# The first body of a hybrid RG-LRU and convolution block: the pair of ma in front of xa

## The reference

```python
h = concatenate([meta, x])                       # 16 + 512 tokens
hn = rms_norm(h, norm_g)
xa, sa, vb, gb, sb, ma, mb = split(hn @ w_in)
ya = rg_lru(causal_depthwise_conv(xa, conv_a_w, conv_a_b), w_rg, b_rg, w_ig, b_ig, lam) * silu(sa)
yb = silu(layer_norm(causal_depthwise_conv(vb * sigmoid(gb), conv_b_w, conv_b_b))) * silu(sb)
merged = sigmoid(ma) * (ya @ w_proj_a) + sigmoid(mb) * (yb @ w_proj_b)
out = rms_norm(h + merged @ w_out)[:, 16:]       # the meta tokens are dropped again
```

## Time and profile before

| what | value |
| --- | --- |
| median of 3 runs | 1765.79 us (1765.69 to 1770.24) |
| the profiled execution | 1768.35 us, of which the span from first to last instruction is 1766.5 us |
| TensorE busy with matmuls | 99% of the span |
| VectorE, ScalarE, GpSimd busy | 74%, 49%, 17% |
| mean granted TensorE clock | 0.995 of full |

### The profile page before, as it was taken

The page is one execution under the profiler, slowest core; times in us unless marked ns, Lnnn a source line. Parts: engine busy times, 40 slices in busy tenths (PEclk is TensorE's granted clock), DMA queues, the critical chain, the costliest instruction groups (busy, mean ns, idle before and its releaser), DMA issues.

```text
span 1766.5 us, 26382 instructions
## 1 busy us (share of the span) xinstructions
PE 1742.7 (99%) x10796; PEld 1574.0 (89%) x10796; DVE 1313.7 (74%) x1561; ACT 867.7 (49%) x1106; POOL 298.0 (17%) x331
## 2 busy tenths in 40 slices
PE   9899999999999999999999999999999999998998
PEld 8899999999999988888888888888888888887886
DVE  7969888888888888788878777898633297764431
ACT  6556555565565523555565555555422264433322
POOL 0502213112222100111211111222100111110000
PEclk9999999999999999999999999999999999999999
DMA  6247768567686665877765767785767679757422
GB/s 208 78 126 167 180 161 178 147 153 178 163 174 147 149 183 146 211 212 219 208 171 160 199 167 211 189 216 177 231 223 232 183 201 203 164 149 262 150 83 95
DMA packets 285656, 311.55 MB, mean 176 GB/s; under 512 B 9440, under 2 KB 239968, under 8 KB 284384
## 3 DMA queue, kind: packets, MB, share of 16 engines
q1 hardware_dynamic: 211024, 188.21, 33.9%
q0 software_dynamic: 74512, 121.65, 31.7%
HBM read 235.38 MB, written 45.09 MB: 159 GB/s over the span
## 4 chain that ended last, share of the span: by engine, by line
PE 93%; DVE 3%; issue 2%; DMA 1%; ACT 1%; POOL 0%; SPq 0%; DVEq 0%; POOLq 0%; ACTq 0%
PE psum L889 28%; PE psum L798 25%; PE psum L759 17%; PE psum L802 13%; PE psum L981 7%; PE psum L995 3%; PE psum L856 1%; DMA t_parts<-m_spill 1%; DVE t_parts L1823 0%; DVE region L1914 0%; DMA region<-in_x_channels 0%; DVE region L1537 0%; DVE x_parts L1698 0%; DVE w_lo L1691 0%; DVE total L1579 0%
## 5 line engine op out<-in xcount | busy, mean ns | idle before, releaser
L1225 ACT ACTIVATE w_hi<-raw 128x1024 fp32r<-128x1024 f32 x110 | 116.3, 1057 | 283.8 <-PE psum L759 137.0
L1471 DVE SCALAR_TENSOR_TENSOR region<-region,params 128x512 f32<-128x512 f32 x368 | 250.6, 746 | 0.0
L1691 DVE TENSOR_TENSOR w_lo<-raw,w_hi 128x1024 fp32r<-128x1024 f32 x110 | 134.9, 1227 | 127.5 <-ACT w_hi L1225 127.5
L889 PE MATMUL psum<-x_parts,w_hi 128*128 128x264 f32 x1792 | 227.1, 284 | 0.0
L889 PEld LDWEIGHTS psum<-x_parts,w_hi 128*128 128x128 f32 x1792 | 222.0, 188 | 0.0
L1698 DVE TENSOR_TENSOR w_lo<-region,w_hi 128x1024 fp32r<-128x1024 f32 x108 | 131.9, 1223 | 70.4 <-ACT w_hi L1241 70.2
L1698 DVE TENSOR_TENSOR x_parts<-region,x_parts 128x1024 fp32r<-128x1024 f32 x108 | 131.7, 1223 | 57.9 <-ACT x_parts L1241 57.9
L889 PE MATMUL psum<-x_parts,t_parts 128*128 128x264 f32 x1344 | 167.9, 284 | 0.0
L889 PEld LDWEIGHTS psum<-x_parts,t_parts 128*128 128x128 f32 x1344 | 165.2, 188 | 0.0
L798 PE MATMUL psum<-t_parts,x_parts 128*128 128x512 f32 x576 | 144.7, 393 | 1.4 <-ACT aux L1285 1.4
L798 PE MATMUL psum<-t_parts,w_hi 128*128 128x512 f32 x576 | 144.9, 393 | 0.2 <-ACT aux L1279 0.2
(11 more groups left out here) (221 smaller groups left out, 3106.4 us busy)
## 6 DMA issues: line engine op xcount, KB each, us to landing
raw<-in_w_in SPq DMA_DIRECT2D x112, 512.0 KB, 4.1
region<-in_w_in SPq DMA_DIRECT2D x56, 1024.0 KB, 6.3
wide<-region POOLq DMA_DIRECT2D x98, 256.0 KB, 5.0
region<-in_w_proj_b SPq DMA_DIRECT2D x16, 1024.0 KB, 8.5
raw<-in_w_out SPq DMA_DIRECT2D x32, 512.0 KB, 4.0
raw<-in_w_proj_a SPq DMA_DIRECT2D x31, 512.0 KB, 4.3
region<-in_w_in POOLq DMA_DIRECT2D x28, 512.0 KB, 7.6
sigmoid_spill<-wide POOLq DMA_DIRECT2D x16, 512.0 KB, 3.3
```

The costliest lines, as they stand in the source:

```text
L889: last = pe.matmul(psum[:, bank + h, 0:HALF], weights[:, k // 2, (k % 2) * P:(k % 2 + 1) * P], part[:, KH * half + k, h * HALF:(h + 1) * H ...
L1225: act.activation(cut_at(n)[0], raw_at(n).rearrange("p (k n) -> p k n", k=4), ACT.Copy).then_inc(hi_ready, 1)
L1471: ins = dve.scalar_tensor_tensor(conv_b[:, t, :], moved, w, conv_b[:, t, :], ALU.mult, ALU.add)
L1691: dve.tensor_tensor(lo, raw_at(n).rearrange("p (k n) -> p k n", k=4), hi.bitcast(F32), ALU.subtract).then_inc(lo_ready, 1)
```

## The change

On SyncE the first tile of x is loaded alone, ahead of the parameters and of the first weight chunk; tile 1, tiles 2 and 3, and then the meta tokens follow behind that chunk. The order of the weight chunks becomes ma, xa, gb, vb. On TensorE chunks 0 to 3 are ma over the 512 tokens (banks 4 and 5), chunks 4 to 7 are xa over all 528 tokens (banks 0 to 3), and the meta tokens' averaging matmul moves from the warm-up to behind chunk 0. On ScalarE and VectorE the meta tokens' steps are spread among the cuts and squares of chunks 0 to 2. The first low cut on VectorE is that of chunk 0, right behind tile 0. `unscaled_xa` waits for chunk 7 and stands behind the low cut of chunk 7; ma's scaling waits for chunk 3.

```diff
@@ SyncE
+        second_loaded = sem("second_loaded")
-                    if x_too and p < 4:
-                        for n in (2 * p, 2 * p + 1) if p else (0,):
+                    if x_too and 0 < p < 4:
+                        for n in (2 * p, 2 * p + 1):
                             sp.dma_start(channels[:, 2 * n:2 * n + 2, :], x_channels[:, 2 * n:2 * n + 2, :])\
                                 .then_inc(x_loaded[n], 16)
...
                     if x_too and p == 0:
+                        sp.dma_start(channels[:, 1, :], x_channels[:, 1, :]).then_inc(second_loaded, 16)
                         sp.dma_start(channels[:, 2:4, :], x_channels[:, 2:4, :]).then_inc(x_loaded[1], 16)
+                        sp.dma_start(meta_x, meta_channels).then_inc(meta_loaded, 16)
...
-            sp.dma_start(meta_x, meta_channels).then_inc(meta_loaded, 16)
+            sp.dma_start(channels[:, 0, :], x_channels[:, 0, :]).then_inc(x_loaded[0], 16)
             sp.dma_start(params[:, :, :], parameters).then_inc(params_loaded, 16)
-            body(0, [c for col in (COL_XA, COL_MA, COL_GB, COL_VB) for c in columns(w_in_v, col)], x_too=True)
+            body(0, [c for col in (COL_MA, COL_XA, COL_GB, COL_VB) for c in columns(w_in_v, col)], x_too=True)
@@ TensorE
             def first_body():
+                for g in range(4):
+                    multiply(0, g, x_tokens((4, 5)), g, raw_x=True)
+                    if g == 0:
+                        pe.wait_ge(meta_summed, 1)
+                        pe.matmul(psum[:, 6, 0:META], average[:, :], stats[:, 0:META], start=True, stop=True)\
+                            .then_inc(meta_mean, 1)
                 pe.wait_ge(meta_lo, 1)
                 for g in range(4):
-                    multiply(0, g, all_tokens(((0, 1), (2, 3))), g, raw_x=True)
-                for g in range(4):
-                    multiply(0, 4 + g, x_tokens((4, 5)), g, mean=g == 0)
+                    multiply(0, 4 + g, all_tokens(((0, 1), (2, 3))), g, mean=g == 0)
...
             for n in range(WARM_UP):
-                if n == WARM_UP // 3:
-                    pe.wait_ge(meta_summed, 1)
-                    pe.matmul(psum[:, 6, 0:META], average[:, :], stats[:, 0:META], start=True, stop=True)\
-                        .then_inc(meta_mean, 1)
                 pe.matmul(psum[:, 7, 0:P], average[:, :], average[:, :], start=True, stop=True)
@@ ScalarE
-                raw_tiles(range(0, 2))
+                raw_tiles(range(0, 1))
+                cut_hi(0, 0)
+                raw_tiles(range(1, 4))
+                act.wait_ge(meta_loaded, 16)
+                act.activation(meta_squares, meta_x, ACT.Square).then_inc(meta_squared, 1)
+                raw_tiles(range(4, 8))
+                square_tiles(range(0, 4))
+                cut_hi(0, 1)
+                act.wait_ge(meta_mean, 1)
+                act.activation(psum[:, 6, 0:META], psum[:, 6, 0:META], ACT.Sqrt, bias=eps).then_inc(meta_rms, 1)
+                raw_tiles(range(8, 12))
+                square_tiles(range(4, 8))
                 act.wait_ge(meta_normed, 1)
                 act.activation(x_hi[:, :, 0:META], meta_x, ACT.Copy).then_inc(meta_hi, 1)
-                cut_hi(0, 0)
-                raw_tiles(range(2, 8))
-                square_tiles(range(0, 4))
-                cut_hi(0, 1)
-                raw_tiles(range(8, 12))
-                square_tiles(range(4, 8))
                 cut_hi(0, 2)
@@ VectorE (sum_meta, norm_meta and cut_meta_lo hold the instructions that stood at L1960 to L1971)
                 for p in range(4):
                     for j in range(4 * p, 4 * p + 4):
+                        if j == 1:
+                            cut_lo(0, 0)
                         dve.wait_ge(raw_x_hi, j + 1)
...
-                    cut_lo(0, p)
                     if p:
+                        cut_lo(0, p)
                         add_squares_of(range(max(4 * p - 4, 1), 4 * p))
+                    if p == 0:
+                        sum_meta()
+                    elif p == 1:
+                        norm_meta()
+                    elif p == 2:
+                        cut_meta_lo()
...
+                cut_lo(0, 7)
                 unscaled_xa()
-                cut_lo(0, 7)
...
-                group_done(0, 8)
+                group_done(0, 4)
                 for t in range(2):
                     dve.tensor_tensor(psum[:, 4 + t, :], psum[:, 4 + t, :], total[:, :], ALU.mult)\
...
             def unscaled_xa():
-                group_done(0, 4)
+                group_done(0, 8)
```

More of the change, by code:

```diff
@@ L1028, in raw_tiles @@
                 for j in tiles:
-                    act.wait_ge(x_loaded[j // 2], 16)
+                    act.wait_ge(second_loaded if j == 1 else x_loaded[j // 2], 16)
                     act.activation(x_hi[:, j, META:T], channels[:, j, :], ACT.Copy,
@@ L1363, in _ @@
             act.activation(stats[:, 33:34], eps, ACT.Sqrt)
[L1364 to L1367, removed]
             act.wait_ge(params_loaded, 16)
@@ L1563, in add_squares_of, with sum_meta, norm_meta, cut_meta_lo @@
                         dve.tensor_tensor(total[:, :], total[:, :], squares(j), ALU.add).then_inc(x_summed, 1)
+                def sum_meta():
+                    dve.wait_ge(meta_squared, 1)
+                    dve.tensor_reduce(stats[:, 0:META], meta_squares.rearrange("p j m -> p m j"), mybir.AxisListType.X,
+                                      ALU.add).then_inc(meta_summed, 1)
+                def norm_meta():
+                    gains = params[:, :, NORM_G:NORM_G + 1].broadcast_to([P, CT, META])
+                    dve.wait_ge(meta_rms, 1)
+                    one_step(dve.reciprocal(psum[:, 6, 0:META], psum[:, 6, 0:META]))
+                    one_step(dve.tensor_tensor(meta_x, meta_x, psum[:, 6:7, 0:META].broadcast_to([P, CT, META]),
+                                               ALU.mult))
+                    dve.tensor_tensor(meta_x, meta_x, gains, ALU.mult).then_inc(meta_normed, 1)
+                def cut_meta_lo():
+                    dve.wait_ge(meta_hi, 1)
+                    dve.tensor_tensor(x_lo[:, :, 0:META], meta_x, x_hi[:, :, 0:META].bitcast(F32), ALU.subtract)\
+                        .then_inc(meta_lo, 1)
                 for p in range(4):
                     for j in range(4 * p, 4 * p + 4):
+                        if j == 1:
+                            cut_lo(0, 0)
                         dve.wait_ge(raw_x_hi, j + 1)
@@ L1959, in _ @@
             dve.memset(eps, EPS).then_inc(eps_ready, 1)
-            dve.wait_ge(meta_squared, 1)
-            dve.tensor_reduce(stats[:, 0:META], meta_squares.rearrange("p j m -> p m j"), mybir.AxisListType.X,
-                              ALU.add).then_inc(meta_summed, 1)
             dve.wait_ge(params_loaded, 16)
[L1964 to L1971, removed]
             first_body()
```

## The result

The changed kernel took **1775.07 us** in the median of 6 runs (1774.22 to 1776.88), the kernel before beside it 1765.78 us (6 runs). The ratio is 1.0050, 95% interval 1.0040 to 1.0061: slower by 9.3 us in the medians, where +9.5 us and 1775.3 us were forecast. The profiled execution took 1774.83 us, its span is 1773.0 us.

The account below looks back on a forecast made before the run. VectorE was taken to set the pace up to chunk 11, TensorE's matmuls after it. +7.8 us (later convolution) + 1.7 us (half clock behind chunk 11) = +9.5 us on 1765.79: 1775.3 us, chance 0.5, range 1769.5 to 1778.5 us.

Parts of the forecast that it names:

- What bounds the kernel: First body: VectorE sets the pace up to chunk 11; any delay of chunk 11's start is paid in full.
- Part 1: Start: first matmul 1.5 us earlier, at 9.1 us; ScalarE's cut of chunk 1 not earlier, 16.2 us against 16.14.
- Part 2: VectorE from chunk 1's cut: meta tokens' steps delay the last addition of squares 1.6 us, to 40.1 us; bounds 0, 2.2.
- Part 3 and 4: TensorE to chunk 7, then convolution: chunk 7 ends at 60.5 us; convolution and chunk 11 +7.8 us, bounds 5.0, 8.8.
- Part 5: Behind chunk 11: TensorE idles 2.7 us before it, then the clock falls to half, costing 1.7 us; bounds 0, 1.7.
- (a): Behind chunk 11: no fall of the clock, +7.8 us, 1773.6 us; chance 0.23.
- (b): From 17.2 us TensorE runs through, not held by VectorE's additions: +5.0 us, 1770.8 us; chance 0.09.
- (c): After 60 us: later convolution meets less of GpSimd, up to 4.5 us come back: +3.3 us, 1769.1 us; chance 0.09.
- (d): Up to chunk 11 TensorE's stream sets the time, not xa's copy: -3.2 us, 1762.6 us; chance 0.03.
- (e): Before the first gate round: 5.9 us idle delays weight chunks or ScalarE's queue further, +12, 1778 us; chance 0.06.

Follow-up runs that it names:

- experiment 2: Kernel before; only the copy of xa moved behind chunk 7's low cut and made to wait for chunk 7: 1773.57 us, ratio 1.0042.
- experiment 8: Kernel before, unchanged, profiled again: 1765.46 us.
- experiments 7: Changed kernel with 15 small matmuls in TensorE's 4.5 us idle hole near 1592 us (the late hole): 1774.26 us, ratio 1.0041.
- experiment 10: Changed kernel with 15 small matmuls in TensorE's hole before the first gate round: 1776.37 us, ratio 1.0053.
- 6: Kernel before with 15 small matmuls in TensorE's 4.5 us idle hole near 1592 us (the late hole): 1765.16 us, ratio 0.9991.
- 9: Kernel before, unchanged, profiled once more: 1767.37 us.
- 11: Kernel before; ma's scaling and sigmoid moved behind chunk 11's cuts, last normed tile's low cut moved from GpSimd to VectorE: 1766.66 us, ratio 0.9998.
- (4): Changed kernel, copy of xa reading ma's banks (no wait for chunk 7) and put ahead of chunk 7's low cut: 1768.63 us, ratio 1.0012.
- (3): Changed kernel, copy of xa reading ma's banks, so waiting for chunk 3 only, still behind chunk 7's low cut: 1770.35 us, ratio 1.0022.
- experiment 1: Kernel before with only the ma and xa pairs exchanged, copy of xa behind chunk 7; loads and meta steps as before: 1773.96 us, ratio 1.0042.
- experiment 5: Kernel before with only the new start: tile 0 loaded alone, first weight chunk ahead of tile 1, chunk 0's low cut behind tile 0: 1766.71 us, ratio 1.0006.
- experiment 12: Kernel before with 11's edits, 26 warm-up matmuls for 18, 11 small ones before the third gate round, late hole filled: 1765.60 us, ratio 0.9996.

## Why the prediction came out right, and where it was wrong inside

**What bounds the kernel** was read rightly: a delay of the convolution of xa is paid in full. Against the first profile, the convolution moved by 61.91 - 54.36 = 7.55 us and chunk 11 by 7.44; and a wait alone, put in front of the copy (experiment 2), cost most of what the exchange costs. Against the undisturbed profile of the kernel before (experiment 8), the earliest of all, chunk 11 moved by 93.36 - 83.97 = 9.4 us.

**Part 1, the start.** Right that ScalarE's cut of chunk 1 does not gain: 15.88 us, where the undisturbed profile of the kernel before even has it at 14.90. But two misses cancelled in it. The cut of chunk 0 began at 7.46 us, below the lower bound of 7.7, so that the first matmul came at 8.56 us, not 9.1; and ScalarE then waited 0.5 us for tiles of x, for which 0.2 were put. Wrong was that TensorE would idle as long as before ahead of chunk 0 and that the clock would fall in it: the warm-up matmuls lasted until 8.1 us in this execution, the idle time was 0.44 us (1.53 and 1.61 us in the profiles of experiments 7 and 10), and no profile of the changed kernel shows a lower clock before 60 us. It would have been covered either way.

**Part 2, the meta tokens on VectorE.** 1.6 us were put on the stretch to the last addition. The row of that addition is at 38.94 + 0.69 = 39.63 us after, with the stretch begun at 16.95: 22.7 us against 21.25 before, +1.4 us. Right. The exchange alone, without these steps, took 1.1 us less than the whole change in the medians, where the theory gave 1 to 1.5; the intervals of the two, some 2 us on either side, overlap.

**Part 3 and 4, chunk 7 and the convolution.** The average was forecast for 40.1 us and stood at 39.69; the copy for 60.6 and stood at 60.42; the convolution for 62.2 and began at 61.91; the first gate round for 66.4 and began at 65.95. Chunk 11 was forecast for 93.7 us and began at 93.36. The steps hold to 0.5 us, each a little early. Against its own base, the first profile, the forecast of +7.8 us came out as 93.36 - 85.92 = +7.4.

**Part 5, the clock behind chunk 11: the term that failed.** 1.7 us were put there and nothing of the kind is in any profile of the changed kernel. (The half clock in chunk 8 came as forecast: its high pass took 6.04 us against 4.06 before.) The forecast idle time of 2.7 us did not appear: chunk 10 began at 84.95 us, not 84.1, and in the profile it ran 7.61 us at a partly lower clock, as before. It began late because GpSimd's lot of low cuts in front of it took longer, 7.17 us against 6.08. Its timelines, before and after:

```profile
70.16 6.08 POOL L670 TENSOR_TENSOR x_parts<-region,x_parts 128x512 fp32r<-128x512 f32 x4 [4.72 <-ACT x_parts L1043]
```

```profile
77.68 7.17 POOL L673 TENSOR_TENSOR x_parts<-region,x_parts 128x512 fp32r<-128x512 f32 x4 [4.72 <-ACT x_parts L1045]
```

Nor did the idle time appear where chunk 10 ran at full clock, in the changed kernel with the late hole filled: 0.20 us before the last gate round and 1.14 us before chunk 11. Where chunk 10 began early, in experiment 10 (GpSimd's lot took 6.11 us there), it ran at the lower clock. An early chunk 10 at full clock, which the term needs, is in none of the three profiles.

**What stands in its place is the base.** The sum was made against one execution whose front was slow: x there later, and the clock down in chunk 0. TensorE then ran without a pause from 10.58 us to the average at 39.32, while VectorE's last addition was done at 38.47, so that the late and slow chunk 0 was paid in full up to there. The prediction saw that lower clock, took 1.7 us as its price (chunk 0 took 5.63 us against 4.13 at full clock, 1.5 us), and assumed it for every run. It also saw that this execution was 2.6 us above the median, and put its shift on the median all the same, since an early shift would be the same in each. That step failed: what made this execution slow lay in good part in the very front that the change replaces. In the undisturbed profile the average comes at 37.40 us, and everything up to chunk 11 is 1.95 us earlier; the late hole gives the other 0.9 us of the difference between the two.

The front of the changed kernel varies as well, if less. In the six profiles with the old front (experiments 2, 6, 8, 9 and 11 and the first) the average comes between 37.39 and 39.32 us, 38.2 in the mean; in the five with the new one between 39.18 and 40.22, 39.7 in the mean. That is +1.4 us, where the first pair of profiles shows +0.4. The new front has no such good case, since the average waits for VectorE's additions, and these have the meta tokens' steps among them. With the stretch behind the average, 7.1 us longer in the table below, the sum is +8.5 us. It fits the 8.4 to 8.8 us against the larger sets of runs, and lies inside the interval of the 9.3.

So the forecast of 1775.3 us was met with one term of 1.7 us that was wrong and one that was missing, of 1.0 us in the mean and 1.95 against the best profile; and the base of 1765.79 us was 0.5 to 0.9 us below the medians of the larger sets. That these nearly cancel is luck. A slow and a quick front both occur in the kernel before; how often each does was not counted.

**Where the time is.** The last column leaves out how early the front of an execution was: it is the time from the average to chunk 11, against 46.6 us in all four profiles of the kernel before, the filled one included.

| kernel | the average | chunk 11 begins | between them |
| --- | --- | --- | --- |
| undisturbed, before (experiment 8) | 37.40 us | 83.97 us | 46.6 us |
| changed, no wait, copy first (4) | 39.18 us | 85.88 us | 46.7: +0.1 |
| changed, no wait, copy behind the cut (3) | 39.84 us | 88.03 us | 48.2: +1.6, the order of copy and cut |
| before, with the wait alone, and that order (2) | 38.98 us | 91.41 us | 52.4: +5.8 |
| pairs exchanged alone (1) | 37.23 us | 90.87 us | 53.6: +7.0 |
| the whole change | 39.69 us | 93.36 us | 53.7: +7.1 |

The 1.2 us between the wait alone and the exchange are the longer chunks: behind the average stand three and a third of 528 tokens where 512 had been, at 5.87 us instead of 5.53 (an estimate from the earlier trace rows: 1.1 us).

**The rivals.** (a) had the right event, no fall behind chunk 11, and its 1773.6 us were 1.5 us off for the reason above. (b) was out: chunk 7 ended at 60.4 us, not 57.7. Behind 17 us TensorE waited 0.64 us for a tile's low cut by VectorE and 0.36 us for ScalarE's cut of chunk 4; ScalarE had waited 3.60 us for VectorE's additions just before that cut. (c) did not occur: the low cut of the second gate round took 1.52 us again (1.53 in the earlier trace rows), for GpSimd's steps moved with VectorE's. One later cut did come free (0.42 us at 81.08 us, where it was stretched before), worth 1.1 us, but GpSimd's lot beside it took 1.1 us longer (part 5), and chunk 10 waited for that. (d), the other side, was tested by experiment 5 and gained nothing. (e) did not occur.

The Trainium skill (TensorE: Matmul & The Clock Gate, section "HAM oscillation") blames only long waits of TensorE for the lower clock. Here waits of 2.36 and 2.88 us before chunk 0, short ones by that section's rule, were followed by the lower clock, those of 1.59 and 1.70 us were not; the trace does not agree with the Trainium skill here, and the rows decide.

## What to carry to other kernels

A result that a long serial chain hangs on should be computed first, even where that makes the first matmul later: here the pair that could start 0.7 to 2 us sooner was the one nobody waited for, and the reader of the other began 9.6 to 11.5 us later. Ask of each exchange who reads the later one, and when that reader used to get to it. And before a sum is made against one profile, look whether its front has idle time or a low clock that need not be in every execution; a second profile of the same kernel would have shown 1 to 2 us of difference.

## What the runs showed of the hardware that was not expected

- The same program's first transfers differ from execution to execution: the first weight and x tiles let chunk 0 begin at 9.05, 9.29, 9.51, 9.53, 10.24 and 10.58 us in six profiles of kernels with the same front.
- In the first body the granted clock fell from 2.4 to 1.2 GHz behind single waits of TensorE of 1.86, 2.24, 2.36, 2.88, 3.0 to 3.3 and 5.6 us, and in chunk 10 twice behind two waits close together (0.48 and 1.53 us in the changed kernel, 0.74 and 1.51 us in experiment 2). It did not fall behind single waits of 1.59, 1.70 and 2.14 us, nor behind 1.51 and 1.52 us close together (experiment 1). So the length of the waits alone does not sort the cases; what does was not found. In the late hole, of 4.5 us, the slow stretch behind it cost between 1.5 and 2.8 us (sixteen matmuls in 5.27 to 6.62 us against 3.79 at full clock). Fifteen small matmuls in the hole removed it.
- More clock is not more speed: the kernel with a mean clock of 0.998 to 0.999 was no faster than those at 0.996, as the stretches that it sped up in the first body were covered or came back as waits (experiment 12).
